# Expert inputs gathered as quarter rows on four partition groups and turned by VectorE instead of TensorE

## The reference, cut to what matters

```python
# x: 2048 tokens x 1024, float32; everything below is float32
h = x + token_mixer(rms_norm(x, norm1_w))      # not touched by the change
u = rms_norm(h, norm2_w)
gp = softmax(u @ w_group + b_group)            # 4 groups, the best one is taken
el = (u @ w_router + b_router) of that group   # 8 experts in it, the best 2 are taken
gate = softmax(the two logits) * the group's weight
for e in range(32):                            # tokens of expert e: about 128 of 4096 assignments
    y = (silu(u_e @ w_gate[e]) * (u_e @ w_up[e])) @ w_down[e]   # 1024x512, 1024x512, 512x1024
    h[tokens of e] += gate * y
out = rms_norm(h, final_norm_w)
```

## Time and profile before

| | |
|---|---|
| median of 3 runs | 1798.38 us (1797.32 to 1799.09) |
| the profiled execution's own time | 1797.4 us |
| its span, first to last instruction | 1795.1 us |
| mean granted TensorE clock | 0.989 |
| PE busy | 1733.0 us, 97% |
| DVE, ACT, POOL busy | 37%, 29%, 22% |
| DMA, all queues | 317.79 MB, 177 GB/s over the span |
| slices 25 to 39 of 40 (the experts) | PE 9 of 10, DMA 8 to 9 of 10 |

### The profile page before, as it was taken

How to read it: one execution, slowest core, us unless ns; L and a number is a source line. 1 busy time by engine, 2 the same in 40 slices (tenths; PEclk the granted TensorE clock), 3 DMA queues, 4 the chain that set the end, 5 groups by cost and what they waited for, 6 DMA issues and landing times. The chain is left out here.

```text
span 1795.1 us, 31916 instructions
## 1 busy us (share of the span) xinstructions
PE 1733.0 (97%) x11402; PEld 1292.1 (72%) x11403; DVE 662.1 (37%) x1720; ACT 512.2 (29%) x1333; POOL 387.5 (22%) x522
## 2 busy tenths in 40 slices
PE   6899999999999999999978999999999999999996
PEld 5677676766667676676746778788778888878784
DVE  1344345533454344544457222222223222222222
ACT  1444424444344333443333111111111111111111
POOL 0001010000100011010100334343434343434333
PEclk9999999999999999999989999999999999999998
DMA  9411011111110011100123889889999899999994
GB/s 355 111 59 37 25 59 58 43 35 39 58 58 35 23 58 58 58 35 23 58 78 133 270 275 354 309 299 332 331 329 346 302 327 326 345 305 352 327 316 139
DMA packets 135208, 317.79 MB, mean 177 GB/s; under 512 B 19413, under 2 KB 23738, under 8 KB 135172
## 3 DMA queue, kind: packets, MB, share of 16 engines
q1 hardware_dynamic: 109540, 261.93, 42.3%
q0 software_dynamic: 24768, 55.26, 8.7%
q10 hardware_dynamic: 864, 0.10, 0.0%
HBM read 286.79 MB, written 59.77 MB: 193 GB/s over the span
## 5 line engine op out<-in xcount | busy, mean ns | idle before, releaser
L303 PE MATMUL bank<-uT,w_in_sb 128*128 128x128 f32 x2304 | 277.2, 279 | 2.3 <-DVE uT L647 2.3
L303 PEld LDWEIGHTS bank<-uT,w_in_sb 128*128 128x128 f32 x2304 | 268.1, 195 | 11.1 <-issue 8.9
L1279 PEld LDWEIGHTS bank<-xT,wts 128*128 128x128 f32 x2048 | 252.1, 193 | 27.4 <-issue 24.8
L1279 PE MATMUL bank<-xT,wts 128*128 128x128 f32 (+2 forms) x2048 | 257.0, 285 | 7.8 <-issue 4.2
L297 PE MATMUL bank<-w_in_sb,uT 128*128 128x512 f32 (+1 forms) x768 | 261.5, 494 | 0.0
L1292 PE MATMUL bank<-xT,wts 128*128 128x128 f32 (+2 forms) x2048 | 247.9, 282 | 0.0
L1292 PEld LDWEIGHTS bank<-xT,wts 128*128 128x128 f32 x2048 | 245.0, 191 | 0.0
L1320 PE MATMUL bank<-wts,hT 128*128 128x512 f32 x512 | 233.3, 598 | 0.1
L325 PE MATMUL bank<-w_out_sb,mixT 128*128 128x512 f32 x512 | 222.7, 593 | 1.5 <-ACT mixT L521 0.8
L297 PEld LDWEIGHTS bank<-w_in_sb,uT 128*128 128x128 f32 x768 | 127.1, 190 | 110.2 <-issue 110.2
L827 POOL TENSOR_SCALAR ss<-ss 128x1 f32<-128x1 f32 (+1 forms) x49 | 9.4, 191 | 821.2 <-ACT junk L571 439.5
(11 more groups left out here) (255 smaller groups left out, 1880.0 us busy)
## 6 DMA issues: line engine op xcount, KB each, us to landing
wts<-w_gate_in SPq DMA_DIRECT2D x32, 2048.0 KB
wts<-w_up_in SPq DMA_DIRECT2D x32, 2048.0 KB
wts<-w_down_in SPq DMA_DIRECT2D x32, 2048.0 KB, 10.9
x_sb<-x_in SPq DMA_DIRECT2D x17, 512.0 KB, 3.6
xT_in<-x_t_in SPq DMA_DIRECT2D x17, 512.0 KB, 4.3
w_in_sb<-w_in_in SPq DMA_DIRECT2D x4, 2048.0 KB, 12.0
h_sb<-x_in SPq DMA_DIRECT2D x16, 512.0 KB, 3.3
h_dram<-h_sb SPq DMA_DIRECT2D x16, 512.0 KB, 2.9
```

The source lines that it names most:

```text
L303: m = pe.matmul(bk[name][0:hi - lo, col:col + P], w_in[:, k, lo:hi], uT[:, k, :], start=k == 0, stop=k == KD - 1)
L1279: m = pe.matmul(G[m_ % 2][:, 0:w], wg[:, k, m_ * P:(m_ + 1) * P], xT[:, k, 0:w], start=k == 0, stop=k == KD - 1)
```

## The change

The tokens of an expert are gathered as five pieces of 32 tokens. Each piece is one indirect DMA of 128 quarter rows (1 KB each): quarter a of token i lands on partition 32a + i. DVE transposes the 32x32 blocks of that and multiplies by a `norm2_w` in the new order; each of the two steps is done in two halves of the features. PE transposes nothing in the experts, and the weights' rows are stored in the matching order in device memory. The row numbers of all pieces are worked out in the routing. POOL's order becomes: sums put, roots, index copy, five gathers, sums read, output rows put. For the last expert it is roots, output rows, sums. PE puts the tail's matmuls after three of the four steps of the first down half, and the quad matmul right after that half.

```diff
+PIECES = MAIN // TAIL
# routing: PE
-        pe.matmul(bank[3][:, 0:NE], rep[:, 0:P], idx_f[:, :], start=True, stop=True).then_inc(sem("slot_sums"), 1)
+        for t in range(PIECES):
+            m = pe.matmul(bank[3][:, t * NE:(t + 1) * NE], rep[:, t % 4 * P:(t % 4 + 1) * P], idx_f[:, t // 4, :], start=True, stop=True)
+        m.then_inc(sem("slot_sums"), 1)
# experts: POOL
+    def copy_pieces(po, n):
+        wait_apart(po, idx_rider, (sem("m_xg_taken"), n + CREDIT))
+        nc.gpsimd.tensor_copy(idxm[:, :], idxq[:, PIECES * n:PIECES * n + PIECES] ...)
...
+    def gather(po):
+        for t in range(PIECES):
+            po.indirect_dma_start(out=xq[:, t * CAP:(t + 1) * CAP], in_=quarters(scratch["v2"]), out_offset=None,
+                                  in_offset=bass.IndirectOffsetOnAxis(ap=idxm[:, t:t + 1], axis=0)).then_inc(sem("m_xg_loaded"), 16)
     def move(po, n, last=False):
         wait_apart(po, idx_rider, (sem("base_loaded"), 32 * n + 32), (sem("rows_put"), 32 * n))
         rows_of(po, 6 * n + 6)
         wait_apart(po, idx_rider, (sem("move_index_ready"), n + 2))
+        if last:
+            roots(po, n)
+            put_out(po, n)
+            put_sums(po, n)
+            return
         put_sums(po, n)
         roots(po, n)
-        if not last:
-            wait_apart(po, idx_rider, (sem("sums_put"), 32 * n + 32), (sem("scaled"), 2 * n + 2))
-            gather_base(po)
+        copy_pieces(po, n + 2)
+        gather(po)
+        wait_apart(po, idx_rider, (sem("sums_put"), 32 * n + 32), (sem("scaled"), 2 * n + 2))
+        gather_base(po)
         put_out(po, n)
# experts: PE
+    def pe_chunk(pe, n, w):
+        main = slice(0, P)
+        pe_gate(pe, "m_", n, w)
+        pe_up(pe, "m_", n, w)
+        wait(pe, sem("m_w_down_loaded"), 16 * (n + 1))
+        after(pe, "m_", "summed", 3 * n - 1)
+        after(pe, "m_", "h_ready", 4 * n + 3)
+        pe_down(pe, YB[0], n, 0, main, range(KF - 1))
+        after(pe, "m_", "h_ready", 4 * n + 4)
+        if w > P:
...
+            m.then_inc(sem("m_d_done"), 1)
+        pe_down(pe, YB[0], n, 0, main, range(KF - 1, KF)).then_inc(sem("m_d_done"), 2 if w == P else 1)
+        if w > P:
+            after(pe, "m_", "tail_square", n + 1)
+            pe.wait_ge(sem("fw_loaded"), 6 * 16)
+            pe.matmul(U[0][:, 0:2], quad[:, :], part[:, :], start=True, stop=True)
+        after(pe, "m_", "summed", 3 * n)
+        pe_down(pe, YB[1], n, 1, main, range(KF)).then_inc(sem("m_d_done"), 1)
# experts: DVE
+    def dve_x(v_, n):
+        wait(v_, sem("m_xg_loaded"), 16 * PIECES * (n + 1))
+        after(v_, "m_", "u_done", 4 * n)
+        for half in range(2):
+            ks = slice(4 * half, 4 * half + 4)
+            nc.vector.transpose(xT[:, ks, 0:MAIN].rearrange("p k (t j) -> p t k j", j=TAIL),
+                                xq.rearrange("p (t k i) -> p t k i", t=PIECES, k=KD)[:, :, ks, :]).then_inc(sem("m_xg_turned"), 1)
+            wait(v_, sem("m_xg_turned"), 2 * n + half + 1)
+            m = nc.vector.tensor_tensor(xT[:, ks, 0:MAIN], xT[:, ks, 0:MAIN], norm2q[:, ks].unsqueeze(2).to_broadcast([P, 4, MAIN]), ALU.mult)
+            m.then_inc(sem("m_xT_ready"), 1)
+        v_.sem_inc(sem("m_xg_taken"), 1)
# DVE block, per expert
                 dve_h(v_, "m_", e)
-                dve_x(v_, e + 1, range(2))
+                dve_x(v_, e + 1)
                 dve_tail(v_, e)
-                dve_x(v_, e + 1, range(2, 3))
                 dve_sums(v_, e)
                 dve_scale(v_, e)
# POOL block
-            for e in range(2):
-                copy_index(po, "m_", e, 2 * e)
-                gather(po)
+            copy_pieces(po, 0)
+            gather(po)
...
             first_base(po)
+            copy_pieces(po, 1)
+            gather(po)
             with po.Fori(0, NE - 1) as e:
-                copy_index(po, "m_", e + 2, 2 * e + 4)
-                gather(po)
                 move(po, e)
```

More of the change, by code:

```diff
@@ L1216, in scatter_over @@
         put_back(po, y[:, 1, :], 1)
[L1218 to L1222, removed]
     def gather_over(po):
@@ L1228, in gather_over, with copy_index @@
                 .then_inc(sem("o_xg_loaded"), 16)
[L1230 to L1247, removed]
+    def copy_index(po, n, col):
+        wait_apart(po, idx_rider, (sem("o_x_done"), 4 * n + CREDIT))
+        nc.gpsimd.tensor_copy(idxc[:, :], idx[:, bass.ds(col, 2)]).then_inc(sem("o_index_ready"), 1)
+        wait_apart(po, idx_rider, (sem("o_index_ready"), n + 1))
     def pe_x_over(pe, n, steps):
@@ L1255, in pe_x_over @@
             for kk in range(2):
-                c = slice((2 * j + kk) * P, (2 * j + kk + 1) * P)
                 for part in range(2):
-                    m = pe.transpose(XB[j % 2][:, kk * CAP + part * P:kk * CAP + (part + 1) * P], xg[:, part, c], ident)
+                    for a in range(4):
+                        m = pe.matmul(XB[j % 2][a * TAIL:(a + 1) * TAIL, kk * CAP + part * P:kk * CAP + (part + 1) * P],
+                                         xg[:, part, a * CAP + (2 * j + kk) * TAIL:a * CAP + (2 * j + kk + 1) * TAIL], ident,
+                                      start=True, stop=True)
             m.then_inc(sem(pre + "x_done"), 1)
@@ L1266, in pe_gate @@
                     after(pe, pre, "summed", 3 * n - 2)
-                    after(pe, pre, "xT_ready", 3 * n + (3 if w > P else 1))
+                    after(pe, pre, "xT_ready", 2 * n + 1)
                 else:
@@ L1293, in pe_up, with pe_down @@
             m.then_inc(sem(pre + "u_done"), 1)
[L1295 to L1303, removed]
+    def pe_down(pe, bank_, n, half, rows, ks):
+        for k in ks:
+            m = pe.matmul(bank_[:, :], hT[:, k, rows], wd[:, k, half * 512:(half + 1) * 512], start=k == 0, stop=k == KF - 1,
+                          skip_group_check=True)
+        return m
+    def pe_chunk(pe, n, w):
[8 more added lines that the diff above has]
+        if w > P:
             for k in range(KF):
@@ L1307, in pe_chunk, with pe_chunk_over @@
                                   start=k == 0, stop=k == KF - 1, skip_group_check=True)
[L1308 to L1313, removed]
-        for half in range(2):
[L1315 to L1327, removed]
+            m.then_inc(sem("m_d_done"), 1)
[6 more added lines that the diff above has]
+        pe_down(pe, YB[1], n, 1, main, range(KF)).then_inc(sem("m_d_done"), 1)
+    def pe_chunk_over(pe, n):
+        pe_gate(pe, "o_", n, CAP)
+        pe_up(pe, "o_", n, CAP)
+        wait(pe, sem("o_w_down_loaded"), 16 * (n + 1))
+        after(pe, "o_", "h_ready", 4 * n + 4)
+        for half in range(2):
+            m = pe_down(pe, G[half], n, half, slice(P, CAP), range(KF))
+        m.then_inc(sem("o_d_done"), 1)
+        for half in range(2):
+            after(pe, "o_", ("yA_taken", "yD_taken")[half], 2 * n)
+            pe_down(pe, YB[half], n, half, slice(0, P), range(KF)).then_inc(sem("o_d_done"), 1)
     def act_silu(act, pre, n):
@@ L1617, in _ @@
             rt_pe(pe)
-            pe_x(pe, 0, range(3))
             rt_pe_last(pe)
```

89 lines of the change are left out of this document (44 added, 45 removed).

## The result

In the first runs the changed kernel took **1948.88 us** (median of 4, 1942.43 to 1953.70) beside 1798.55 us of the kernel before: ratio 1.0839, 95% interval [1.0819, 1.0859]. The forecast was 1799 us, its range 1778 to 1816. It is wrong by 150 us.

The account below looks back on a forecast made before the run. TensorE, busy 99.9%, bounds the kernel, with about 1 us of slack in POOL's loop, which then limits the gain. 1797.4 - 6.5 (experts) + 1.5 (start) + 1.8 + 3.5 (clock) + 0.9 (end) = 1798.6, so 1799 us; range 1778 to 1816.

Parts of the forecast that it names:

- No cost: TensorE before the down projection: without transposes, three first-half steps (2.6 us) still hide VectorE's last product.
- POOL's loop: POOL's turn from sums put to the next sums put: 23.4 us, more than a narrow expert's 21.5.
- P to B: On POOL, from sums put to sums read: 10.8 us instead of 8.7, with all five gathers in between.
- The five gathers land before that: The gathers were claimed to land before the limits that the read sums set, so they would not hold the gate.
- P + 19.2: Earliest next-but-one gate, 19.2 us after POOL puts the sums, set by the sums' read and the tail's sum.
- two clock terms: TensorE at half clock after gaps: one loss at the start, +1.8 us, and two from stalls, +3.5 us.
- Rival 1: Landings of sums and output rows get quicker, PE sets the time: 1784 us, or 1772 to 1776; chance 0.30.
- B to M: On POOL, from sums read to the output rows' landing: forecast to stay near 11.4 us.
- Rival 2: POOL's DMA queue: gathers ahead of the sums' read make it and the output rows land later; 1813 us, chance 0.20.
- Rival 3: DMA becomes the bound, narrow experts take 22.9 us: 1797 to 1801 us; chance 0.05.
- Rival 4: POOL's output-row issues and VectorE's SBUF products hold each other up, at most 0.4 us a loop: 1809 us; chance 0.07.
- main case: TensorE's savings are mostly lost to POOL's turn: 1799 us, own range 1791 to 1809; chance 0.38.

Follow-up runs that it names:

- hand-made lateness: Changed kernel with each expert's third h product held until POOL has issued its nine indirect DMAs and a memset: 1934.17 us, ratio 1.0777 to the kernel before.
- first profile: Profile of the unedited changed kernel from the first runs, span 1951.9 us; those runs had a median of 1948.88 us.
- undisturbed runs: The changed kernel, not edited, run later on three chips: 1797.71, 1798.71 and 1797.12 us, ratios 1.0017, 1.0017 and 1.0016 to the kernel before.
- second profile: Later profile of the unedited changed kernel, on the chip where it took 1797.71 us; span 1796.2 us.
- faster version: Changed kernel with its five gathers moved ahead of the sums' writes: 1775.12 us (0.9898), and again 1776.52 us (0.9909) against the kernel before.

## Why the prediction was wrong

*The step that failed against the first runs* is "No cost", of the wait for VectorE's last product once the transposes are gone: a term put at nothing. It took for granted that a signal arrives when its instruction ends, and gave three steps of 0.86 us as cover. In the first runs TensorE's signals came up to 6 us late while POOL issued its row, the transposes and the 1 us of slack in the order before them were gone, and the bare wait took 82 us of TensorE, and the down projection itself another 44 (280.1 us of busy time on L1303 instead of 236.3), as the granted clock fell to 0.92 to 0.98 in the stages with these waits. The shares of the late `w_up` and of the second products were not measured. Of the rivals none said this. The hand-made lateness shows the price; what made the signals late is not settled. What speaks for and against: in the first profile the third or fourth product starts 1.5 to 1.9 us after the end of POOL's row in 30 of 32 experts, also in the last (released at 1927.04, the row ended at 1925.47), where no weight load is issued behind 1907.92, so the load of `w_gate` is not it. Yet rows of nine on four chips delayed nothing, and the kernel before, without such a row, had late updates in its first profile as well. A condition of that chip or session, which the row makes worse, fits all of it; it could not be brought about again. As both first traces also lack records that all fifteen later ones have, something in how that session recorded its executions is a rival that was not tested.

*Against the undisturbed runs*, point by point:

- TensorE: right within 0.1 us. 21.5, 25.2 and 26.9 us were forecast, 21.50, 25.26 and 26.90 are seen where nothing else holds. With two or three gathers the file takes 1770 us, 24 and 26 less than the kernel before, though it then also moves fewer bytes.
- VectorE's transpose: 0.84 us (66, from 836 to 847 ns) and the product 0.82, forecast 0.85 each.
- The start: the first gate at 991.68, forecast 990.18 + 1.5.
- POOL's loop: P to B right (11.08 for 10.8), the turn 0.9 us too long, and the wait that sets the gate wrong. "The five gathers land before that" is the step that failed. Taken alone it is true, for VectorE has the last gather at P + 16.5 and the limit was P + 19.2. But that is 3.1 us after VectorE is free for it, and 3.24 us of transposes and products and 0.48 of the tail's sum stand behind it in the same queue, which makes P + 20.3, so the next gate hangs on the landing and not on the read sums.
- The sum: -6.5 us was forecast for the experts, -1.2 with the two clock terms (+1.8 and +3.5), which fall in the same stretch. From the first gate to the last the second profile takes 767.2 us, the kernel before on the same chip 766.8: +0.4. That this is near is luck in part: narrow experts after a wide one take 21.8 to 23.2, on the mean 0.8 more than the 21.5 of the forecast, while those that follow a narrow one take 22.1 to 23.1, less than its 23.0 to 23.4.
- Rival 1 (landings get quicker) half happened: in the nine turns in which M ended last, B to M is 10.2 to 11.3, on the mean 10.7, instead of 11.4. It did not set TensorE free, since the gathers' landing held the gate at almost the same length of turn. Rival 2 had the right queue and the wrong DMA: not the read was late behind the gathers, but the gathers themselves. Rival 3 holds in neither: DMA 0.92, and 0.97 in the faster version, which is near it.
- Rival 4: in the version with gathers first, the issues of output rows that fall beside VectorE's transposes and products take up to 1.66 us instead of 1.02, on the mean 0.1 more (1.11 against 1.01 in the first of the two runs). All 16 of them over 1.15 us lie beside a product. That is more than the 0.2 of the earlier trace rows at its longest and less than the whole 0.8; VectorE's own times do not move.
- A slip of adding: "0.30 and a quarter of the main case" is 0.395, not 0.38.

So 1799 us was near the time on those chips (a change of +0.6 us was forecast, +2.0 to +3.6 were measured) by a sum with a wrong link in it. The run with the gathers last exposed the link: its expectation was built on it and missed by 310 us.

## What to carry over

Where an in-order engine's queue holds a wait for a fetch ahead of work that others need, price the fetch's landing as a loop of its own, from what frees or orders its issue to what stands behind the wait. Put fetches as early as their buffer allows, ahead of the writes that only the next turn needs. And when a result is far from the sum, run the unedited kernel again on another chip, and compare the semaphore updates with their instructions' ends, having first counted whether any are missing, before building theories on one profile.

## What was not expected of the hardware

- TensorE's semaphore updates stood up to 6.3 us behind the end of their matmuls in one session; in fifteen later profiles, on five chips, no engine's update was over 0.08 us behind.
- Nine indirect DMAs of 128 rows, issued 1.3 us apart, delay no signal and no product by themselves (1803.6 us with such rows in the kernel before, 1797.7 in the changed one).
- The last of five quarter gathers has 6.65 us from its issue to the transposes that wait for it (1304.94 to 1311.59) while a weight load is under way: the landing, not the issue, was the term to price.
- GpSimd's issues of output rows took up to 1.66 us instead of 1.02 beside VectorE's products of two SBUF tensors, which kept their 0.82 us.
